# Forty instead of thirty-two tokens taken out of the dense expert layers of a two-block model kernel

## The reference, cut to what matters

```
def peer_ffn(h, w_pq, sub_keys, u_tab, v_tab):
    q = (hf @ w_pq).reshape(T, PEER_HEADS, 2, PEER_HALF)
    s = jnp.einsum('thpc,hpnc->thpn', q, sub_keys)
    s1, i1 = lax.top_k(s[:, :, 0], PEER_TOPK)
    s2, i2 = lax.top_k(s[:, :, 1], PEER_TOPK)
    cand = (s1[..., :, None] + s2[..., None, :]).reshape(T, PEER_HEADS, PEER_TOPK * PEER_TOPK)
    best, ci = lax.top_k(cand, PEER_TOPK)
    expert = (e1 * N_KEYS + e2).reshape(T, PEER_HEADS * PEER_TOPK)
    gate = jax.nn.softmax(best, axis=-1)
    ...
    u = jnp.take(u_tab, ec, axis=0)
    act = jax.nn.gelu(jnp.einsum('cd,ckd->ck', hc, u), approximate=False) * gc
    vv = jnp.take(v_tab, ec, axis=0)
    return jnp.einsum('ck,ckd->cd', act, vv)
```

## Time and profile before

| | |
|---|---|
| median of three runs | 3494.09 us (3488.45 to 3501.89) |
| profiled execution | 3497.36 us, of which the span is 3495.5 us |
| mean granted TensorE clock | 0.986 |
| TensorE busy | 3333.4 us (95%) |
| VectorE busy | 2570.6 us (74%) |
| ScalarE busy | 1585.0 us (45%) |
| GpSimd busy | 132.9 us (4%) |
| DMA | 658.29 MB, mean 188 GB/s |

### The profile page before, as it was taken

One profiled execution on the slowest core, in us unless ns is written; L12 is line 12 of the kernel. 1 busy time (PEld: TensorE's weight loads), 2 busy tenths in 40 slices (PEclk: granted clock), 3 DMA queues, 4 the chain that ended last, 5 costly groups with the idle time before them and its releaser, 6 DMA issues.

```text
span 3495.5 us, 68612 instructions
## 1 busy us (share of the span) xinstructions
PE 3333.4 (95%) x24838; PEld 2970.8 (85%) x24838; DVE 2570.6 (74%) x4511; ACT 1585.0 (45%) x2501; POOL 132.9 (4%) x122
## 2 busy tenths in 40 slices
PE   8999999999999899988888899899999999999998
PEld 6888788888888787777777789799999999999998
DVE  6766587776868778766665686877787777777786
ACT  5445444444444455533334422454544445454543
POOL 0000000000000000000000001101011000100000
PEclk9999999999999999999999999999999999999999
DMA  5534545555565444420003445578788887878774
GB/s 196 176 133 167 170 154 173 190 175 196 173 197 182 159 153 139 143 88 12 6 27 109 163 147 176 202 235 309 255 311 273 285 289 266 294 257 307 241 245 161
DMA packets 175003, 658.29 MB, mean 188 GB/s; under 512 B 19744, under 2 KB 28064, under 8 KB 165280
## 3 DMA queue, kind: packets, MB, share of 16 engines
q1 hardware_dynamic: 159744, 559.15, 48.0%
q0 software_dynamic: 15104, 97.03, 7.7%
HBM read 637.99 MB, written 17.04 MB: 187 GB/s over the span
## 4 chain that ended last, share of the span: by engine, by line
PE 75%; DVE 12%; DMA 8%; ACT 3%; issue 2%; SPq 0%; DVEq 0%; ACTq 0%
PE bank L612 42%; PE bank L614 21%; PE bank L950 5%; DMA raw<-in_v_tab 4%; DVE w_lo L1988 3%; PE bank L1248 2%; DMA rows<-in_u_rows,expert_of 1%; DVE hot_row L2899 1%; ACT w_hi L1329 1%; DVE rows L2914 1%; DMA raw<-in_u_tab 1%; DVE hot_col L2894 1%; DVE h_tok L2922 1%; PE bank L635 1%; DVE proj L2546 1%
## 5 line engine op out<-in xcount | busy, mean ns | idle before, releaser
L612 PE MATMUL bank<-h_two,w_hi 128*128 128x512 f32 (+1 forms) x5360 | 1823.5, 390 | 52.7 <-DVE w_lo L1988 21.3
L614 PE MATMUL bank<-h_two,w_lo 128*128 128x256 f32 (+1 forms) x5360 | 1467.4, 274 | 0.0
L1988 DVE TENSOR_TENSOR w_lo<-raw,w_hi 128x1024 fp32r<-128x1024 f32 (+1 forms) x1054 | 1228.1, 1184 | 225.9 <-ACT w_hi L1329 223.9
L1329 ACT ACTIVATE w_hi<-raw 128x1024 fp32r<-128x1024 f32 (+1 forms) x1054 | 1046.3, 1024 | 499.5 <-PE bank L614 254.9
L612 PEld LDWEIGHTS bank<-h_two,w_hi 128*128 128x128 f32 x5360 | 1009.4, 188 | 240.0 <-issue 42.6
L614 PEld LDWEIGHTS bank<-h_two,w_lo 128*128 128x128 f32 x5360 | 1019.4, 190 | 1.1 <-issue 0.7
L612 PE MATMUL bank<-p_two,w_hi 128*128 128x448 f32 x1792 | 571.6, 377 | 5.8 <-DVE acc L2013 5.8
L614 PE MATMUL bank<-p_two,w_lo 128*128 128x224 f32 x1792 | 476.6, 266 | 0.0
L612 PEld LDWEIGHTS bank<-p_two,w_hi 128*128 128x128 f32 x1792 | 337.1, 188 | 40.5 <-DVE w_lo L1988 8.5
L614 PEld LDWEIGHTS bank<-p_two,w_lo 128*128 128x128 f32 x1792 | 343.1, 191 | 0.0
L1334 ACT ACTIVATE stage<-bank 128x256 f32<-128x256 f32 (+1 forms) x242 | 89.0, 368 | 416.7 <-PE bank L614 416.6
(11 more groups left out here) (402 smaller groups left out, 3256.0 us busy)
## 6 DMA issues: line engine op xcount, KB each, us to landing
raw<-in_u_tab SPq DMA_DIRECT2D x256, 512.0 KB
raw<-in_v_tab SPq DMA_DIRECT2D x256, 512.0 KB
raw<-in_w_up SPq DMA_DIRECT2D x176, 512.0 KB
raw<-in_w_in SPq DMA_DIRECT2D x174, 512.0 KB
raw<-in_w_out SPq DMA_DIRECT2D x64, 512.0 KB
raw<-in_w_down SPq DMA_DIRECT2D x64, 512.0 KB
raw<-in_w_pq SPq DMA_DIRECT2D x32, 512.0 KB
gates<-g_stage POOLq DMA_DIRECT2D x14, 896.0 KB, 5.8
```

The costliest lines, as they stand in the source:

```text
L612: nc.tensor.matmul(o[:, 0:2 * width].rearrange("p (a t) -> p a t", a=2), wh, pair[:, :, 0:width], start=(k == 0), stop=False)
L614: last = nc.tensor.matmul(o[:, width:2 * width], wl, pair[:, 0, 0:width], start=False, stop=(k == nk - 1))
L1329: nc.scalar.activation(w_hi[c % 2][:, at:end], raw[c % 2][:, at:end], ACT.Copy).then_inc(hi_done, 1)
L1988: nc.vector.tensor_tensor(w_lo[c % 2][:, at:end], raw[c % 2][:, at:end], w_hi[c % 2][:, at:end].bitcast(F32), ALU.subtract).then_inc(lo_do ...
```

## The change

`TD` goes from 224 to 216, `TG` from 32 to 40, `KQ` from 4 to 3 (3 x 40 = 120 partitions, `PQ`), `GATHERS` from 32 to 43 (the last has one slot more than there are, with gate zero). Operations on rows run on 120 partitions. `OPS_IN` puts rows into first halves too (4) and 9 into second halves. `EARLY` goes from 12 to 10, `EARLY_EXP` from 11 to 7; the last two `scores3` stand behind the halves of whole tile 0; six whole tiles run in the loop of 54 iterations instead of four in one of 56. Gates are stored after every 12 tokens. The GELU of the gathered products moves behind first half 3 on ScalarE, its product with the gates to the first use on VectorE. The turned sums use two banks.

```
-TD = 224
+TD = 216
 TG = T - TD
 KQ = P // TG
-GATHERS = SLOTS // KQ
+PQ = KQ * TG
+GATHERS = -(-SLOTS // KQ)
+GATE_T = 12
-OPS_IN = (0, 10, 0, 11, 0, 11, 0, 10, 0, 10, 0, 8, 0, 4)
+OPS_IN = (4, 9, 4, 9, 4, 9, 4, 9, 4, 9, 4, 9, 4, 4)
...
-        EARLY, EARLY_EXP = 12, 11
+        EARLY, EARLY_EXP = 10, 7
-        SPLIT_AT, LOWER_AT = (40, 51), (44, 55)
+        SPLIT_AT, LOWER_AT = (40, 51), (44, 53)
...
-            for u in (6, 7):
-                scores3(u)
+            pe.wait_ge(drained, N_PQ + DT - 1)
             for x in range(EARLY):
-                whole_tiles(x, 0, DT)
+                whole_tiles(x, 0, DT // 2)
+                if x == 0:
+                    scores3(6)
+                whole_tiles(x, DT // 2, DT)
+                if x == 0:
+                    scores3(7)
...
-                if n < DT:
+                if n < 8 * (DT - EARLY):
                     whole_tiles(EARLY + n // 8, 2 * (n % 8), 2 * (n % 8) + 2)
-                elif n < 3 * DT:
-                    whole_tiles(EARLY + 1 + n // DT, n % DT, n % DT + 1)
...
+            first_layer(3)
             act.wait_ge(best_ready, 2)
-            nc.scalar.activation(act_of[:], dots[:, 0, :], ACT.Gelu).then_inc(gate_exp, 1)
-            with act.Fori(3, PEER_G - 2) as g:
+            nc.scalar.activation(act_of[0:PQ, :], dots[0:PQ, 0, :], ACT.Gelu).then_inc(gate_exp, 1)
+            second_splits(3)
+            with act.Fori(4, PEER_G - 2) as g:
...
-            for b in range(TD // 16):
-                pool.wait_ge(gates_copied, 8 * (b + 1))
+            for b in range(TD // GATE_T):
+                pool.wait_ge(gates_copied, GATE_T // 2 * (b + 1))
...
-            def rows_behind(g, t):
-
-                at = ROWS_USED[2 * g + 1]
-                for n in range(2 * OPS_IN[2 * g + 1]):
-                    if (n * DT + DT // 2) // (2 * OPS_IN[2 * g + 1]) == t:
-                        gathered_rows(at + n // 2, n % 2)
+            def rows_behind(x, t):
+
+                for n in range(2 * OPS_IN[x]):
+                    if (n * DT + DT // 2) // (2 * OPS_IN[x]) == t:
+                        gathered_rows(ROWS_USED[x] + n // 2, n % 2)
...
                         for t in tiles:
                             gated_lower(t, g, p_hi[:, t, :], p_lo[:, t, :])
-                    if g == 3 and i == 0:
-                        dve.wait_ge(gate_exp, 2)
-                        nc.vector.tensor_tensor(act_of[:], act_of[:], gate_of[:], ALU.mult).then_inc(best_ready, 1)
+                        rows_behind(2 * g, c)
```

More of the change, by code:

```diff
@@ L382, in build @@
         sb("under_p_two", [P, DT // 2, 2, TD], F32R, at=top_at)
-        g_stage = [sb(f"g_stage{j}", [P, PEER_G - 1, 16, K_TOP], at=top_at) for j in range(2)]
+        g_stage = [sb(f"g_stage{j}", [P, PEER_G - 1, GATE_T, K_TOP], at=top_at) for j in range(2)]
         top_at.close()
@@ L1308, in sums_turned @@
                 for t in range(DT):
-                    last = nc.tensor.matmul(bank[7][:, t * TG:(t + 1) * TG], y_tok[:, t * P:(t + 1) * P],
-                                            count[:, P + 3 * K_TOP:P + 3 * K_TOP + TG], start=True, stop=True)
+                    last = nc.tensor.matmul(bank[6 + t // 8][:, t % 8 * TG:(t % 8 + 1) * TG], y_tok[0:PQ, t * P:(t + 1) * P],
+                                            count[0:PQ, P + 3 * K_TOP:P + 3 * K_TOP + TG], start=True, stop=True)
                 last.then_inc(peer_turned, 1)
@@ L1941, in _ @@
                 pool.dma_start(h_tok[TG * q:TG * (q + 1), :], h_tok[0:TG, :]).then_inc(k_swapped, 16)
-            pool.wait_ge(slots_done, 3)
+            pool.wait_ge(slots_done, 5)
             for q in range(KQ):
@@ L1961, in gather @@
                 nc.gpsimd.indirect_dma_start(
-                    out=rows[n % 2][:], out_offset=None, in_=a["u_rows" if n < GATHERS else "v_rows"],
-                    in_offset=bass.IndirectOffsetOnAxis(ap=expert_of[:, of:of + 1], axis=0)
+                    out=rows[n % 2][0:PQ, :], out_offset=None, in_=a["u_rows" if n < GATHERS else "v_rows"],
+                    in_offset=bass.IndirectOffsetOnAxis(ap=expert_of[0:PQ, of:of + 1], axis=0)
                 ).then_inc(rows_loaded[n % 2], 16)
@@ L2881, in _ @@
                                     ).then_inc(slots_done, 1)
-            own = slice(P - TG, P)
-            nc.vector.scalar_tensor_tensor(tok_expert[own, :], slot[own, 0, TT - 1, :], float(P), slot[own, 1, TT - 1, :],
-                                           ALU.mult, ALU.add).then_inc(slots_done, 1)
+            for at, end, of in ((0, SLOTS, 0), (SLOTS, KQ * GATHERS, 2 * SLOTS - KQ * GATHERS)):
+                own, here, there = slice(64, P), slice(at, end), slice(of, of + end - at)
+                nc.vector.scalar_tensor_tensor(tok_expert[own, here], slot[own, 0, TT - 1, there], float(P),
+                                               slot[own, 1, TT - 1, there], ALU.mult, ALU.add).then_inc(slots_done, 1)
             dve.wait_ge(slots_done, 1)
-            nc.vector.tensor_copy(tok_gate[own, :], slot[own, 2, TT - 1, :]).then_inc(slots_done, 1)
+            nc.vector.tensor_copy(tok_gate[own, 0:SLOTS], slot[own, 2, TT - 1, :]).then_inc(slots_done, 1)
+            nc.vector.memset(tok_gate[own, SLOTS:KQ * GATHERS], 0.0).then_inc(slots_done, 1)
             dve.wait_ge(turned_copied, 6)
@@ L2907, in gathered_rows @@
                 dve.wait_ge(rows_loaded[n % 2], 16 * (n // 2 + 1))
[L2908 removed]
+                got, of = rows[n % 2][0:PQ, :], n % GATHERS
                 half = slice(D // 2 * x, D // 2 * (x + 1))
@@ L2913, in gathered_rows @@
                 if n < GATHERS:
-                    last = nc.vector.tensor_tensor_reduce(got, got, h_tok[:, half], 1.0, 0.0, ALU.mult, ALU.add,
-                                                          dots[:, x, of:of + 1])
+                    last = nc.vector.tensor_tensor_reduce(got, got, h_tok[0:PQ, half], 1.0, 0.0, ALU.mult, ALU.add,
+                                                          dots[0:PQ, x, of:of + 1])
                 else:
@@ L3002, in _ @@
                         dve.wait_ge(peer_turned, 7)
-                        nc.vector.tensor_tensor(xT[:, :, TD:T], xT[:, :, TD:T],
-                                                bank[7][:].rearrange("p (k t) -> p k t", t=TG), ALU.add)
+                        for k in range(2):
+                            x = xT[:, 8 * k:8 * k + 8, TD:T]
+                            nc.vector.tensor_tensor(x, x, bank[6 + k][:, 0:8 * TG].rearrange("p (k t) -> p k t", t=TG),
+                                                    ALU.add)
                     renewed(i * 2 + (N_END - WHOLE - DT + j + 1), i * 2 + j, TD)
```

30 lines of the change are left out of this document (17 added, 13 removed).

## The result

The kernel became slower: 3657.47 us in the median of six runs (3639.95 to 3676.33) against 3499.28 us for the kernel before, ratio 1.0451 (95% interval 1.0429 to 1.0472). The forecast was 3445 us, with a range to 3472.

The account below looks back on a forecast made before the run. TensorE's pace was taken to bound the halves, VectorE the loop ahead. Gains of 25.7 + 5 + 18.5 = 49.2 us took 3497.4 to 3448.2 us profiled, 3445 us median; range 3424 to 3472.

Parts of the forecast that it names:

- the term on DMA: Second halves with 9 gathers: 25.6 MB in 78.6 us, 326 GB/s, said to fit barely.
- more gathers: 43 instead of 32 per table, row operations beside TensorE in both kinds of halves: a gain taken as 5 us.
- first halves without cover: Rival, chance 0.05: 56 row operations in first halves lie on the path, 68 us; 19 us slower, 3513 us.
- the gathers cost by count: Rival, chance 0.13: each gather costs 2.5 us in the halves; loss of 18 instead of gain of 5, 3468 us.
- the 0.5 us that I allowed: Allowance for each of 7 first halves, whose row operations were otherwise said to cost nothing; 3.5 us in all.
- Narrower matmuls: 3840 TensorE steps in the halves each shorten by 6.7 ns: gain 25.7 us, ends 21.5 and 38.4.
- The reason that I gave: The `w_lo` part is held by its weight load, so only the 16 columns of the `w_hi` matmul shorten, 6.7 ns.
- Earlier turning: Ahead of the halves: slots turn 17.2 us earlier, loop 3.3 us shorter, 2 us lost; gain 18.5 us.
- the 2 us of the forecast: Gate loop: the load behind tile 14 lands late, ScalarE late by some 3 us, 2 us lost after buffering.
- the allowance of 5: Gate loop: stores every three iterations cost nothing, with up to 5 us for the range if one is late.

Follow-up runs that it names:

- rows128: The changed kernel with gathers over all 128 partitions instead of 120, row operations staying on 120; 3498.39 us, ratio to the kernel before 0.9996.

## Why the prediction was wrong

**The step that failed** is the term on DMA: "16 x 1.049 MB + 9 x 0.983 MB = 25.6 MB in 78.6 us, 326 GB/s ... It fits barely." It priced a gather of 120 rows by its bytes, 0.983 against 1.049 MB, from rows of gathers over 128 partitions. No row of before showed another partition count, and the part "more gathers" said that fewer partitions don't shorten the row operations without asking what they do to the transfer. They nearly double each packet of a gather, from 309 to 580 ns, and the engines are 0.9 busy at 250 GB/s already: 159 us, measured by `rows128` against the changed kernel. I set no bound on the dear side of that price, and none of my rivals had it. The rival on the slower side, first halves without cover, has a true core, but all row operations together cost 19 us where they are alone (24 by the ratios); it is not what made the changed kernel slow.

**More gathers, a gain of 5.** Also wrong, and hidden behind the first. With whole gathers the price rose from 7 us to 59, a loss of some 50 instead of a gain of 5. The form of the argument was that operations beside TensorE cost nothing as long as each chunk of VectorE fits in 4.9 us, and transfers cost nothing as long as the mean need is under the mean rate. Each falls short alone by 19 and 16 us (24 and 22 by the ratios), and together they cost more than that. The wait for the last reload of the gates, 8.2 us on VectorE, comes from the new place of the gathers, and the sum has no term for it. The sum of bytes also left out the reload of the gates, 1.77 MB in each second half; with it the need was 27.4 MB, 348 GB/s, more than the 323 of the earlier trace rows and the 327 that the fastest window here moved, so "barely" should have been "not". The rival "the gathers cost by count" had this mechanism, and its loss of 18 us was still a third of what was measured. One of its sums doesn't follow from its rows: halves with 10, 11 and 8 gathers that lose 5.8, 2.8 and 0.8 us add up to 24 us over the six halves, so 20 us for the new ones would be 4 less, not 4 more. First halves do pay (80 to 82 us instead of 78.5), against the 0.5 us that I allowed, though not all of that is the row operations' own, which lengthen them to 80.1.

**Narrower matmuls, 25.7 us.** Right in size. A step is 307 ns in the median (forecast 306.7). Without gathers a first half fell from 80.22 to 78.51 us, 1.71 us in 256 steps, 6.7 ns a step. The reason that I gave isn't shown by this. If only the `w_hi` matmul shortened, the whole fall would lie between the starts of `w_hi`'s and `w_lo`'s matmul. Averaged over the undisturbed stretches of the two kernels without gathers, that distance fell from 213.5 to 209.7 ns, and the one from `w_lo` to the next `w_hi` from 101.4 to 98.5 ns. Both parts became shorter, and why their sum comes out as forecast stays open.

**Earlier turning, 18.5 us.** Right about the places, within what was measured. The slots turned at 2130.44 (forecast 2130.9), the split form came at 2229.76 (forecast about 2232); VectorE has its gates without the wait of 21.09 us. In the loop, ScalarE waited 2.50 us for a weight chunk, and TensorE behind it 1.90, the 2 us of the forecast; a late gate store held ScalarE for 6.03 us and TensorE for 4.12, within the allowance of 5. That the split form still came 2 us early means that the rest of the loop was some 6 us faster than I had it. Together the two terms were forecast at 44.2 us and measured at 49.3 without gathers. With gathers only the start of the split form bears the forecast out; in whole times the turning showed 15 us on the kernel before and nothing on `rows128`.

**Sum.** 44.2 + 5 forecast; 49.3 - 52 - 159 measured, each with some microseconds of uncertainty. The first two of these nearly cancel, which is the 0.9996 of `rows128`; the third is the 1.0451.

## What to carry to other kernels

A gather that doesn't fill all 128 partitions may be dearer than one that does; fill the spare ones with any valid row and throw it away. When a change alters the number of partitions of a transfer, its price is unknown until a trace shows it: read the packets' engine time per MB on the queue's line, not the bytes. Two loads that each fit beside the bound engine (a DMA at 0.9 of its time, VectorE at 0.8) can cost more than the sum of their separate prices, so measure them together. A transfer that queues behind one that waits for a buffer waits with it; when gathers move, look at what stands behind them in the same queue.

## What the runs showed of the hardware

A gather's packet of 8 KB took 309 ns over 128 partitions, and 527, 493 and 578 ns over 96, 112 and 120. The DMA engines, 0.9 busy, moved 325 GB/s in a second half with gathers of the first kind and 242 to 254 GB/s with gathers over 120.

A wait can cost TensorE twice. After an idle 3.64 us its steps took 0.57 instead of 0.31 us for some 5 us, and over the 15 halves the granted clock was 0.95 where `rows128` had 0.99. Of the 166 us between these two stretches, TensorE's idle time is 111 us and its longer busy time, 1265.5 against 1210.9 us for the same work, 55. The window of `rows128` over its 15 halves:

```profile
2234.00:3477.00 1243.00, 1210.90 (x7713) 1160.18 (x7713) 975.24 (x1385) 603.49 (x841) 123.74 (x94) 0.99 0.81 283
```
